# Down projection of a feed-forward block as Strassen products on one Trainium2 core

## What is computed

```python
x = x + y @ w_o
h2 = rms_norm(x, g_ffn)
x = x + jnp.square(jax.nn.relu(h2 @ w_up)) @ w_down      # 1024 -> 4096 -> 1024
# second layer
h = rms_norm_2(x, norm_w);  proj = h @ w_in              # begins with u_s, input of the state space branch
mag = jnp.exp(lr * dt); ab_re = mag * jnp.cos(li * dt); ab_im = mag * jnp.sin(li * dt)
# bb = f * b: the tables of the scan depend on parameters alone, not on x
```

## Time and profile before

| | |
|---|---|
| median of 3 runs | 1046.73 us (1046.08 to 1047.77) |
| profiled execution, device time | 1047.61 us |
| its span in the trace | 1045.8 us |
| mean granted TensorE clock | 0.995 |
| busy: PE / DVE / ACT / POOL | 1014.4 / 456.7 / 203.3 / 26.0 us |
| mean DMA rate | 134 GB/s |

### The profile page before, as it was taken

How to read it: one execution, slowest core, us unless ns; L and a number is a source line. 1 busy time by engine, 2 the same in 40 slices (tenths; PEclk the granted TensorE clock), 3 DMA queues, 4 the chain that set the end, 5 groups by cost and what they waited for, 6 DMA issues and landing times.

```text
span 1045.8 us, 11237 instructions
## 1 busy us (share of the span) xinstructions
PE 1014.4 (97%) x4628; PEld 605.4 (58%) x4628; DVE 456.7 (44%) x1018; ACT 203.3 (19%) x407; POOL 26.0 (2%) x39
## 2 busy tenths in 40 slices
PE   5999999999999999999999999999996999999998
PEld 3754444665555459888644459458743444468543
DVE  1502811235677722597060021767783953432111
ACT  3312222223241122102100011001101212353000
POOL 3000000000000004000000000000000000000000
PEclk9999999999999999999999999999998999999999
DMA  9441732244244436444244443442421433411621
GB/s 293 149 164 38 252 113 77 99 143 161 81 122 161 149 117 195 165 161 161 89 153 160 162 145 111 147 161 82 161 96 66 161 134 114 150 45 41 242 81 41
DMA packets 70803, 139.68 MB, mean 134 GB/s; under 512 B 2864, under 2 KB 6208, under 8 KB 70752
## 3 DMA queue, kind: packets, MB, share of 16 engines
q1 hardware_dynamic: 68832, 134.56, 37.4%
q0 software_dynamic: 1712, 4.32, 1.8%
q10 hardware_dynamic: 208, 0.08, 0.0%
HBM read 137.90 MB, written 1.05 MB: 133 GB/s over the span
## 4 chain that ended last, share of the span: by engine, by line
PE 92%; DMA 3%; DVE 2%; ACT 1%; issue 1%; SPq 0%; DVEq 0%; ACTq 0%
PE pair L1382 80%; PE turned L1318 3%; DMA arena<-in_mem 2%; DMA ring<-in_w_in 1%; PE score L1742 1%; PE score L1675 1%; DVE arena L720 1%; PE score L1755 1%; PE score L1487 1%; PE score L1536 1%; PE score L1486 1%; PE score L1552 1%; PE score L1521 0%; PE turned L1662 0%; PE turned L1664 0%
## 5 line engine op out<-in xcount | busy, mean ns | idle before, releaser
L1382 PE MATMUL pair<-ring,hT 128*128 128x512 f32 (+2 forms) x1024 | 445.1, 589 | 9.9 <-ACT arena L664 5.3
L1382 PEld LDWEIGHTS pair<-ring,hT 128*128 128x128 f32 x1024 | 192.1, 192 | 225.2 <-issue 219.2
L720 DVE TENSOR_TENSOR arena<-arena 128x256 f32<-128x256 f32 (+8 forms) x307 | 202.0, 674 | 86.8 <-ACT arena L428 47.7
L1382 PE MATMUL pair<-hT,ring 128*128 128x256 f32 (+2 forms) x1232 | 216.0, 336 | 0.0
L1382 PEld LDWEIGHTS pair<-hT,ring 128*128 128x128 f32 (+1 forms) x1232 | 191.8, 190 | 22.0 <-issue 1.9
L1382 PE MATMUL pair<-ring,arena 128*128 128x512 f32 (+1 forms) x480 | 201.3, 578 | 0.0
L1382 PEld LDWEIGHTS pair<-ring,arena 128*128 128x128 f32 x480 | 90.5, 190 | 103.7 <-issue 102.8
L428 ACT ACTIVATE arena<-pair 128x512 f32<-128x512 f32 (+2 forms) x70 | 39.0, 582 | 203.7 <-PE pair L1382 203.6
L858 DVE CUSTOM_DVE_ANT_0 arena<-score,masks 128x256 f32<-128x256 f32 (+2 forms) x40 | 18.1, 451 | 118.1 <-PE score L1487 66.5
L438 ACT ACTIVATE arena<-turned 128x512 f32<-128x512 f32 (+2 forms) x66 | 32.8, 536 | 164.7 <-PE turned L1318 164.7
L1318 PE MATMUL turned<-ident,arena 128*128 128x128 f32 (+1 forms) x363 | 52.8, 285 | 10.0 <-issue 4.7
(11 more groups left out here) (176 smaller groups left out, 465.4 us busy)
## 6 DMA issues: line engine op xcount, KB each, us to landing
ring<-in_w_in SPq DMA_DIRECT2D x33, 2048.0 KB, 8.8
ring<-in_w_up SPq DMA_DIRECT2D x8, 2048.0 KB, 9.1
ring<-in_w_down SPq DMA_DIRECT2D x8, 2048.0 KB, 8.0
ring<-in_w_o SPq DMA_DIRECT2D x4, 2048.0 KB, 8.1
ring<-in_w_mem_kv SPq DMA_DIRECT2D x2, 2048.0 KB, 8.3
ring<-in_w_glu SPq DMA_DIRECT2D x2, 2048.0 KB, 8.2
ring<-in_w_ssm_out SPq DMA_DIRECT2D x2, 2048.0 KB, 8.8
ring<-in_w_ukv SPq DMA_DIRECT2D x4, 512.0 KB, 4.0
```

Of the source, the lines that this page charges most:

```text
L720: return dve.tensor_tensor(o, a, b, op)
L1382: ins = pe.matmul(o_, s, m, start=a, stop=b, skip_group_check=o.startswith("down"))
```

## The change

The down projection is done by Strassen's scheme. The inner dimension of 4096 is cut into eight groups of 512 rows (jobs `down0` to `down7`, each 512 rows by all 1024 columns, again 2 MB). In each group the activation (256 positions by 512) is cut into quarters a11 to a22 and the weights (512 by 1024) into b11 to b22. VectorE forms four sums of activation quarters (128x256 each) and four of weight quarters (128x1024 each) in `mix(g)`, and TensorE makes seven products, each of two matmuls of 128x512 (`multiply`). Each of the seven products accumulates over the eight groups in a PSUM bank of its own: four in the pairs, the others in the banks of the transposes and scores. Buffers of the sums exist twice (`g % 2`). At the end VectorE combines the seven products into x. As these banks are needed, the scan tables must be out of them by then: the lane parameters are prepared before ScalarE's first `take` and turned between the halves of `up1`, C is turned after `up2`, B after `up5`, and `m0` is made after `up6`. VectorE does its work on C before it squares.

```diff
-T_B = T_LANE + 8
-T_C = T_B + 4
+T_C = T_LANE + 4
+T_B = T_C + 8
...
-    out += [(f"down{h}{k}", f"down{h}", "w_down", DM * k, DM, 512 * h, 512) for k in range(4) for h in range(2)]
+    out += [(f"down{g}", "down", "w_down", 512 * g, 512, 0, DM) for g in range(8)]
...
+    if _job[1] == "down":
+        HALVES.append((_job[0], 1))
...
+        mixed = Place(ff_at + 8192)
+        wmix = [[mixed(1024) for _ in range(3)] for _ in range(2)]
+        rmix = [[mixed(256) for _ in range(4)] for _ in range(2)]
+        assert mixed.at <= a2.at
...
+        first, second = (pair[(OUTS.index("up6") + i) % 2] for i in range(2))
+        product = {1: bank["turned"][0][:, :], 2: first[:, 0:512], 3: first[:, 512:1024], 4: bank["score"][1][:, :], 5: second[:, 0:512],
+                   6: second[:, 512:1024], 7: bank["score"][0][:, :]}
+
+        def quarters(g):
+
+            r = hup[:, 1024 * g:1024 * g + 1024].rearrange("p (k t) -> p k t", t=SEQ)
+            slot = STREAMED.index(JOB[f"down{g}"]) % RING
+            w = ring[:, slot, :].rearrange("p (k n) -> p k n", n=DM)
+            rows = [r[:, 0:2, 0:P], r[:, 2:4, 0:P], r[:, 0:2, P:SEQ], r[:, 2:4, P:SEQ]]
+            weights = [w[:, 0:2, 0:512], w[:, 0:2, 512:DM], w[:, 2:4, 0:512], w[:, 2:4, 512:DM]]
+            s = [x.rearrange("p (k t) -> p k t", t=P) for x in rmix[g % 2]]
+            t = [x.rearrange("p (k n) -> p k n", n=512) for x in wmix[g % 2]]
+            return rows, weights, s, t
...
+            act.wait_ge(sem("ssm_in"), 16 * 9)
+            act.activation(srow[0:ST, 258:260], srow[0:ST, 256:258], ACT.Exp).then_inc(sem("dt_ready"), 1)
+            act.wait_ge(sem("theta"), 1)
+            link(act.activation(R[:, 3, :], R[:, 3, :], ACT.Exp))
+            link(act.activation(R[:, 5, :], R[:, 5, :], ACT.Sin))
+            act.activation(R[:, 4, :], R[:, 4, :], ACT.Sin).then_inc(sem("trig"), 1)
...
             for i in range(8):
                 take(f"up{i}", lambda t: hup[:, 1024 * i + 512 * t:1024 * i + 512 * t + 512], func=ACT.Relu)
                 if i == 0:
...
                 if i == 2:
-                    turned(lane[:, 0:160], 160)
-                if i == 6:
+                    for k in range(4):
+                        turned(c_turned[:, 512 * k:512 * k + 512], 512)
+                if i == 5:
                     act.wait_ge(sem("tables"), 1)
                     for k in range(8):
                         turned(bt[:, 512 * k:512 * k + 512], 512)
-            for k in range(4):
-                turned(c_turned[:, 512 * k:512 * k + 512], 512)
...
-            for i in range(8):
-                dve.wait_ge(sem("taken_act"), taken(f"up{i}")[1])
-                u = hup[:, 1024 * i:1024 * i + 1024]
-                mark(tt(u, u, u, ALU.mult), "ff_ready")
...
+            def ff(i):
+
+                dve.wait_ge(sem("taken_act"), taken(f"up{i}")[1])
+                u = hup[:, 1024 * i:1024 * i + 1024]
+                mark(tt(u, u, u, ALU.mult), "ff_ready")
+
+            def mix(g):
+
+                (a11, a12, a21, a22), (b11, b12, b21, b22), (s1, s2, s3, s4), (t2, t3, t4) = quarters(g)
+                if g >= 2:
+                    dve.wait_ge(sem("half_done"), done(f"down{g - 2}", 1))
+                step(tt(s3, a21, a11, ALU.subtract))
+                link(tt(s1, a21, a22, ALU.subtract))
+                link(tt(s2, a11, s1, ALU.subtract))
+                mark(tt(s4, a12, s2, ALU.subtract), "rows_mixed")
+                n = STREAMED.index(JOB[f"down{g}"])
+                dve.wait_ge(sem(f"weights{n % RING}"), 16 * (n // RING + 1))
+                link(tt(t3, b12, b22, ALU.add))
+                mark(tt(b12, b11, b12, ALU.add), "weights_mixed")
+                link(tt(t2, b12, b22, ALU.add))
+                mark(tt(t4, t2, b21, ALU.add), "weights_mixed")
+
+            for i in range(7):
+                ff(i)
             dve.wait_ge(sem("m0_ready"), 1)
             mark(dve.tensor_copy(m0, m0_bank[:, 0:256]), "m0_taken")
-
-            residual_norm(("down0", "down1"), xn3)
+            dve.wait_ge(sem("turned_taken"), T_B)
+            mix(0)
+            ff(7)
+            for g in range(1, 8):
+                mix(g)
+
+            x = [[xres[:, t, 512 * i:512 * i + 512] for i in range(2)] for t in range(TT)]
+            q1, v, w5 = (hT[:, 2 * i:2 * i + 2, :].rearrange("p k n -> p (k n)") for i in range(3))
+            dve.wait_ge(sem("product"), 1)
+            link(dve.tensor_copy(q1, product[1]))
+            step(tt(x[0][0], x[0][0], q1, ALU.add))
+            dve.wait_ge(sem("product"), 2)
+            link(tt(v, product[6], q1, ALU.subtract))
+            step(tt(x[1][0], x[1][0], v, ALU.subtract))
+            dve.wait_ge(sem("product"), 3)
+            link(tt(w5, product[5], v, ALU.add))
+            step(tt(x[0][1], x[0][1], w5, ALU.add))
+            link(tt(x[1][1], x[1][1], w5, ALU.add))
+            dve.wait_ge(sem("product"), 4)
+            mark(tt(x[0][1], product[3], x[0][1], ALU.add), "residual")
+            dve.wait_ge(sem("product"), 5)
+            mark(tt(x[0][0], product[2], x[0][0], ALU.add), "residual")
+            row_norm(0, xres[:, 0, :], xn3[:, 0:DM], 0, "x")
+            dve.wait_ge(sem("product"), 6)
+            mark(tt(x[1][1], product[7], x[1][1], ALU.add), "residual")
+            link(tt(x[1][0], x[1][0], product[7], ALU.subtract))
+            dve.wait_ge(sem("half_done"), done("down7", 1))
+            mark(tt(x[1][0], product[4], x[1][0], ALU.add), "residual")
+            row_norm(1, xres[:, 1, :], xn3[:, DM:2 * DM], 0, "x")
...
             half_job("up0", 1)
+            R = srow[0:ST, :].rearrange("p (k n) -> p k n", n=128)
+            pe.wait_ge(sem("lane_rows"), 1)
+            turn("lane", [R[:, k, :] for k in (4, 5, 3, 7, 8)])
+            assert n_unit["turned"] == T_LANE, n_unit
             half_job("up1", 1)
-            R = srow[0:ST, :].rearrange("p (k n) -> p k n", n=128)
...
+            def multiply(q, g):
+
+                (a11, a12, _, a22), (b11, b12, b21, b22), (s1, s2, s3, s4), (t2, t3, t4) = quarters(g)
+                rows, weights = {1: (a11, b11), 2: (a12, b21), 3: (s4, b22), 4: (a22, t4), 5: (s1, b12), 6: (s2, t2), 7: (s3, t3)}[q]
+                for k in range(2):
+                    ins = pe.matmul(product[q], rows[:, k, :], weights[:, k, :], start=g == 0 and k == 0,
+                                    stop=g == 7 and k == 1, skip_group_check=True)
+                return ins
+
+            def multiplied(ins, g):
+
+                assert HALVES[finished[0]] == (f"down{g}", 1)
+                finished[0] += 1
+                ins.then_inc(sem("half_done"), 1)
+
             pe.wait_ge(sem("turned_taken"), n_unit["turned"])
-            for j in range(ST):
-                q = slice(32 * (j % 4), 32 * (j % 4) + 32)
-                for i in range(2):
-                    a = 2048 + 1024 * i + 32 * j
-                    ins = pe.matmul(m0_bank[q, 32 * (j // 4):32 * (j // 4) + 32], bx[:, i, j, 1, :], cc[:, a:a + 32], start=i == 0, stop=i == 1)
-            ins.then_inc(sem("m0_ready"), 1)
-            pe.wait_ge(sem("ff_ready"), 8)
-            half_job("down03", 0)
-            half_job("down13", 0)
-            half_job("down03", 1)
-            half_job("down13", 1, 0, 2)
-
+            pe.wait_ge(sem("m0_taken"), 1)
+            for g in range(6):
+                n = STREAMED.index(JOB[f"down{g}"])
+                pe.wait_ge(sem("ff_ready"), g + 1)
+                pe.wait_ge(sem(f"weights{n % RING}"), 16 * (n // RING + 1))
+                multiply(1, g)
+                if g == 0:
+                    by, v = taken("up7")
+                    pe.wait_ge(sem(by), v)
+                multiply(2, g)
+                pe.wait_ge(sem("rows_mixed"), g + 1)
+                multiply(3, g)
+                pe.wait_ge(sem("weights_mixed"), 2 * g + 1)
+                multiply(7, g)
+                multiply(5, g)
+                pe.wait_ge(sem("weights_mixed"), 2 * g + 2)
+                multiply(6, g)
+                multiplied(multiply(4, g), g)
+            for g in (6, 7):
+                n = STREAMED.index(JOB[f"down{g}"])
+                pe.wait_ge(sem(f"weights{n % RING}"), 16 * (n // RING + 1))
+            pe.wait_ge(sem("weights_mixed"), 16)
+            for q in (1, 6, 5, 3, 2, 7):
+                multiply(q, 6)
+                multiply(q, 7).then_inc(sem("product"), 1)
+            multiplied(multiply(4, 6), 6)
 
             pe.wait_ge(sem("x_rows"), 5)
             turn_rows("x", xn3, 0)
-            half_job("down13", 1, 1, 2)
+            multiplied(multiply(4, 7), 7)
```

More of the change, by code:

```diff
@@ L113 @@
 JOB = {job[0]: n for n, job in enumerate(JOBS)}
-OUTS = list(dict.fromkeys(job[1] for job in JOBS))
+OUTS = list(dict.fromkeys(job[1] for job in JOBS if job[1] != "down"))
 LAST_JOB = {job[1]: job[0] for job in JOBS}
 FIRST_JOB = {job[1]: job[0] for job in reversed(JOBS)}
```

(29 more changed lines are left out.)

28 lines of the change are left out of this document (14 added, 14 removed).

## The result

The changed kernel takes 1052.81 us (median of 4 runs, 1052.06 to 1054.31), the kernel before 1047.25 us beside it (4 runs). The ratio is 1.0055, with a 95% interval of 1.0038 to 1.0073: slower by 5.6 us, where +3.5 was forecast. Its profiled execution took 1053.14 us, the span 1051.0, and the mean granted clock fell from 0.995 to 0.987.

A forecast was written before the change was run, and what follows sets the result against it. TensorE, busy for 97% of the span, was taken as the bound. Terms -13.7 + 4.4 + 0.1 + 7.2 + 0.4 + 4.1 + 1.0 = +3.5 took 1046.7 to 1050.2 us; range 1045.0 to 1054.0, the forecast's own 1048.5 to 1052.5.

The forecast's parts named there:

- rival (c): GpSimd's copies delay VectorE fully, both clock penalties are 2.5 us: +5.7 us, 1052.4; slower ring sums up to 1056; 15%.
- 16 matmuls fewer: Down projection: 112 matmuls instead of 128, at the same 0.858 us each, save 13.7 us.
- wait for the lanes: Between the halves of `up1`: TensorE idles from 411.0 to 415.4 until the lane parameters are ready, +4.4 us.
- GpSimd's copies: At the lane parameters: VectorE's earlier chain collides with GpSimd's four copies, +1.0 us, between bounds of 0 and 2.3.
- wait for group 7's sums: Before interleaved groups 6 and 7: TensorE idles while VectorE makes the last sums, which wait for group 5, +7.2 us.
- clock, first stretch: After the idle wait for the lane parameters: TensorE's clock falls to half, +2.05 us, bounds 0 to 2.5.
- clock, second stretch: After the idle wait for group 7's sums: TensorE's clock falls to half, +2.05 us, bounds 1.6 to 2.5.
- transposes, tail: Moved transposes and `m0` cost +0.1 us; turning the normalised tiles at the end of the down projection costs +0.4 us.
- what idle time costs beyond itself: After both new TensorE idle stretches: the clock drops from 2.4 to 1.2 GHz, 2.05 us each, +4.1 us together.
- Rival (a): The clock stays up or soon returns and GpSimd's copies don't collide: 1045.1 to 1046.7 us, same as before; 25%.
- Rival (b): Before groups 6 and 7: the last sums don't hold TensorE; without that wait -5.7 us, 1041, faster; 10%.

The follow-up runs named there:

- late waits: The changed kernel with products 1, 2, 3 of groups 6 and 7 first and the wait for all sums behind them: 1042.37 us, ratio 0.9946.

## Why the prediction was right, and where it was short

The direction, the two idle stretches and what releases them were as forecast. The size, +3.5 against +5.6, was short: 1052.81 us lies inside the whole range but above the forecast's own, 1048.5 to 1052.5, and just above what rival (c) reached by full collision and dear clocks. By its terms, before against after in the traces:

| term | forecast | measured | from |
|---|---|---|---|
| 16 matmuls fewer | -13.7 | -13.7 | 12.01 us a group |
| wait for the lanes | +4.4 | +4.4 | 415.55 - 409.87 = 5.7, less the collision |
| GpSimd's copies | +1.0 | +1.3 | 10.14 against 8.84 us |
| wait for group 7's sums | +7.2 | +7.1 | 596.97 - 589.84 |
| clock, first stretch | +2.05 | +2.7 | 23.49 - 21.07, and 0.25 at the lanes |
| clock, second stretch | +2.05 | +2.7 | 25.05 - 22.35 |
| transposes, tail | +0.5 | +0.5 | 2.33 against 2.27; 2.98 against 2.59 |
| sum | +3.5 | +5.0 | |

409.87 is 395.57 plus two halves of 7.15 us, 21.07 is one such half and the 13.92 us of `up2`, and 589.84 is 588.12 plus two matmuls. The distance from `up0` to `us0` grew by 4.8 in all. The rest of the span differs for reasons outside the change. The changed kernel reached `up0` 1.1 us earlier in its execution. Behind the seam it lost more, at the two old idle stretches. They are as long as before, but in the changed kernel's timeline the work behind them is slower, 9.39 us for 8.52 and 12.50 for 12.06:

```profile
792.19 9.39 PE L1441 MATMUL pair<-ring,hT 128*128 128x512 f32 x16 [5.33 <-ACT arena L684]
...
811.47 1.94 PE L1382 MATMUL turned<-ident,arena 128*128 128x128 f32 x8 [4.75 <-issue]
813.20 12.50 PE L1441 MATMUL pair<-ring,hT 128*128 128x512 f32 x24
```

That is 1.3 us in this execution which no edit made, and 4.8 - 1.1 + 1.3 and some tenths make up the 5.2 us of the span. How much of such differences is in the 5.6 us of the medians was not measured.

The term that was mis-sized is "what idle time costs beyond itself". The step took the mean of two samples from one execution, 1.6 and 2.5, where the two new stretches cost 2.7 each. The old stretches stand unedited in all nine traces, so they show what a sample is worth. By the distance from the start of the resumed work to what follows it, against the same at full clock, the first (5.33 us idle) cost 1.6, 2.5, 2.2, 2.4, 3.2, 2.2, 2.5, 2.6 and 2.6 us, beginning with the kernel before and the changed one and going on in the order of the experiments. The second (4.75 us) cost 2.5, 2.9, 2.8, 2.9, 1.6, 2.8, 2.9, 3.0 and 3.0. The means are 2.4 and 2.7. So the sample of 1.6 was the lowest price of that stretch in nine executions: the way of pricing was right, and the trace it was taken from was unlucky. The two bounds were wrong as well: 0 for a stretch of 4.4 us, where even 1.95 us had its price, and 2.5 at the top, where 3.2 occurs.

Rival (a), that the clock stays up, fell with the 0.50 behind both stretches and with the 1.3 us of the collision. Rival (b), that the last sums don't hold TensorE, fell with the late waits: moving that wait gave 10 to 11 us. Rival (c) was the nearest in time, with both prices of the clock above its 2.5, but not for all its reasons: the collision was 1.3 and not 2.3, and sums on the weights' ring took 1.22 to 1.23 us, as in the arena.

By the Trainium skill, SBUF — State Buffer, section "Who interferes with whom", a VectorE instruction with two inputs from SBUF contends with a GpSimd instruction that reads it, and one of the two waits in full. The trace agrees, one instruction at a time: both two-input sums ended only behind the copy they began beside, and only VectorE waited, since the copies kept their 2.62 us. The prediction read the rule as a wait for all four copies, 2.3 us. But a VectorE instruction came through at each copy's end, so four instructions were stretched and 1.3 us lost.

## What to carry to other kernels

Fewer matmuls pay only where TensorE doesn't wait, so with a scheme that needs sums first, look for a wait with no work ahead of it. Here it was the last round of the double-buffered sums: TensorE asks for them at the very place where it first allows VectorE to begin. Order the work that needs no sums (products 1 and 2 read raw quarters) right behind that place, and ask for the rest late. Price an idle stretch of TensorE as its length plus what the clock costs: 1.6 to 3.2 us in these traces, about 2.6 on average. One or two samples don't give that price. Shortening the stretch saves about the length cut off (3.6 us less idling gained 4.6, 3.5 less gained 2.9); the clock's price was gone where no idle stretch above 0.4 us was left.

## What the runs showed of the hardware

- The price of the lower clock shows no growth with the length of the idle stretch: 1.6 us after 1.95 us idle, 3.0 after 3.45, 2.9 after 4.41, 2.7 after 5.52, 2.1 after 6.83 and 2.7 after 6.97. These are single samples, and the same stretch of 5.33 us cost 1.6 in one execution and 3.2 in another. The clock can also fall after work has resumed, as it did behind the 1.95 us.
- VectorE's one-input TENSOR_SCALAR of 32x128 was slowed beside GpSimd's copies too, 0.58 and 0.64 us instead of 0.21 and 0.22.
- Changing the PSUM bank every two matmuls cost nothing that the trace shows: 0.858 us a matmul as with eight in a row.
